# A two-layer mLSTM / Conformer step with eight experts: the three smallest experts moved into the last pass of the largest

## The chip, the cores and the metric

The kernel runs on one core of a Trainium2 chip. The metric is the device time of one execution in microseconds (us): 1841.56 is the median of three runs (1840.25 to 1843.03). Its engines are TensorE (PE; its weight loads are listed as PEld), VectorE (DVE), ScalarE (ACT), GpSimd (POOL) and SyncE (SP), which issues most transfers from device memory (DMA). Each engine runs its own instructions in order and waits on semaphores.

## What is computed

Two token groups of 128 rows (256 rows of 1024 features) pass through two layers with shared weights. Layer 0 is a bidirectional mLSTM and a dense SwiGLU; layer 1 is a convolution module and a SwiGLU with eight experts. The change concerns the experts:

```python
logits = (t @ w_router).astype(float32)              # t: tokens x 1024
top_v, top_i = lax.top_k(logits, 2)
probs = softmax(top_v)
for e in range(8):                                   # w1[e]: 1024 x 7168, w2[e]: 3584 x 1024
    u = t @ w1[e]
    out += combine[:, e:e+1] * ((silu(u[:, :3584]) * u[:, 3584:]) @ w2[e])
```

The router gives each token to two experts, 512 places in all. Only the rows that an expert was given have to be computed. All weights are float32: gate, up and down of one expert are 3 x 3584 x 1024 numbers, 44.04 MB.

## The kernel before

**Weights.** One expert's weights lie in device memory as 168 rows of 128 x 512 numbers (`EXPERT_ROWS`), in 28 stages of six rows (1536 KB). The hidden width of 3584 is cut into seven groups of 512. In order: 8 rows gate 0, 8 rows up 0, 8 gate 1, 8 up 1, 8 down 0, 8 gate 2, and so on to down 6: 21 blocks of 8 rows. SP loads the stages into `ring`, seven slots of one stage (`expert_stage`, L472).

**An ordinary pass** (`expert(i, False)`) computes one expert for up to 128 tokens. For float32 precision with fast products, each half stage (a cut of three rows) is split: ScalarE writes its rounded part to `w_hi` (L899), VectorE the rest to `w_lo` (L1349), four buffers deep, and TensorE makes three products per row, hi x hi, lo x hi and hi x lo (L1584 to L1586), of 512 columns each. A ring slot is free for the next load when its stage is split. After each group's up block come tanh on ScalarE (L942), two VectorE steps (L1455, L1456), four transposes (L1989), and the split of the hidden values (L949, L1466). The next pass's tokens are gathered by POOL from the buffer `xg` (L577) and transposed (L1910) near the end of a pass.

**Which tokens go where.** VectorE computes counts, ranks and addresses (L1382 to L1410) and the plan (L1426 to L1440). Expert 0 comes first. Of experts 1 to 7 the one with most tokens comes last and may have 192 tokens; an expert with more than its limit gets a further pass. So there are eight passes and one for each overflow.

**The last pass** (`expert(items, True)`) computes the largest expert: 128 tokens in the way above, and 64 more, the side rows, with raw float32 weights from `ring`, without a split: after each block of 8 rows `side_group` multiplies the same 8 rows (L1923), each as two products of 256 columns into the two halves of PSUM's partitions. Here a ring slot is free only when the side rows have used it (`side_rows`). The side's hidden values have their own tanh (L945), VectorE steps (L1460, L1462), two transposes (L1994) and a copy (L952). At the end the side result is copied (L1480) and stored by SP (L504); then POOL fetches each token's two results (L588), and VectorE, ScalarE and POOL combine them and do the final norm.

Of the kernel before, what the change touches and what calls it, by code (L numbers as in the profile page):

```python
# [30 lines left out]
BIG = 1e30  # L31

# [131 lines left out]
ITEMS = EXPERTS + OVER  # L164
SIDE = 64
SMALL = EXPERTS - 1
P_ITEMS, P_EXPERT, P_BIG, P_LOADS, P_ALL = 0, 1, SMALL + OVER, SMALL + OVER + 1, SMALL + OVER + 2
YG_ZERO = SMALL + 2
ZEROED = ITEMS + 1 + ITEMS + 2 - YG_ZERO


def mlstm_conformer_kernel(nc, vecs, consts, rowc, x_in, pos, w_gate, w_router, mix, ff, moe, c0, norm_out,
# [7 lines left out]
    with ctx:  # L180
# [37 lines left out]
        xg = nc.dram_tensor("xg", [(ITEMS + 1) * P, D], f32)  # L218
        yg = nc.dram_tensor("yg", [(ITEMS + 2) * P, D], f32)
# [73 lines left out]
        ranks = carve(7, EXPERTS)  # L293
        one_of = carve(4)
        side_x = carve(KD, SIDE)
        side_th, side_sg, side_tok = carve(ROW // 2), carve(ROW // 2), carve(ROW // 2)
# [11 lines left out]
        more = OVER + 1  # L308
        hit = carve(more, EXPERTS)
        hit_desc = carve(more, EXPERTS)  # L310
        has, who = carve(more), carve(more)
# [23 lines left out]

        hT_lo_end = part("hT_lo", P, KD // 2, T)
        in_hT_hi, in_hT_lo, in_w_hi = ([ring_r[:, b, MIX:STAGE].rearrange("p (k t) -> p k t", t=T) for b in blocks]
# [13 lines left out]
        BIG_UP, SIDE_UP, SIDE_Y = 1, 3, 7  # L351
# [48 lines left out]
        side_in, side_turned, side_x_ready = sem("side_in"), sem("side_turned"), sem("side_x_ready")  # L400
        side_tanh, side_chain, side_done = sem("side_tanh"), sem("side_chain"), sem("side_done")
        side_hid_turned, side_hid_ready = sem("side_hid_turned"), sem("side_hid_ready")
        side_rows = sem("side_rows")
        side_y_ready, side_y_stored = sem("side_y_ready"), sem("side_y_stored")
        xi_in, yg_stored, picked_in = sem("xi_in"), sem("yg_stored"), [sem("picked_in0"), sem("picked_in1")]
# [6 lines left out]
        def slot(n):  # L412
            return n % SLOTS
# [27 lines left out]
        def _(sp):  # L441
# [43 lines left out]
            loads = sp.value_load(plan[0:1, P_LOADS:P_LOADS + 1], min_val=SMALL - 1, max_val=SMALL - 1 + OVER)  # L485
# [7 lines left out]
            big = sp.value_load(plan[0:1, P_BIG:P_BIG + 1], min_val=1, max_val=EXPERTS - 1)  # L493
            for j in range(SLOTS):
                sp.wait_ge(split_ready, loads * CUTS + (FF_CUTS + CUTS + 2 * (j - SLOTS + 1)))
                expert_stage(None, big * FC + j, j)
            for j in range(SLOTS, FC):
                sp.wait_ge(side_rows, ((j - SLOTS) * PER + PER - 1) // KD + 1)
                expert_stage(None, big * FC + j, j)
# [1614 lines left out]
```

## Time and profile before

| | |
|---|---|
| median of three runs | 1841.56 us |
| the profiled execution | 1839.32 us, span 1837.6 us from first to last instruction |
| mean granted TensorE clock | 0.977 |
| busy: TensorE, VectorE, ScalarE | 95%, 74%, 56% of the span |
| read from device memory | 504 MB, mean 284 GB/s |
| stage loads of experts | 224 of 1536 KB |
| expert passes | from 770.46 to 1808.58 us, eight of them |

All durations below come from the one profiled execution. "Busy" for TensorE includes the modelled ends of pipelined products, so distances between starts say more than durations: an L1584 product is shown with 0.39 us, but three products follow each other in 0.68 us. A clock of 1.00 is 2.4 GHz, 0.50 would be 1.2 GHz.

### The profile page before, as it was taken

To read this page: it belongs to the slowest core of one execution; us is meant where nothing else is said; L and a number is where in the kernel's file an instruction comes from. 1 tells how busy PE (TensorE), PEld (TensorE's weight loads), DVE (VectorE), ACT (ScalarE), POOL (GpSimd) and SP (SyncE) were. 2 spreads that over 40 slices of the span, in tenths; PEclk is the share of its full clock that TensorE was granted. 3 is DMA by queue.
4 is the path that set the end of the run, shared out by engine and by line. 5 is a ranking of instruction groups with operands and counts; after the bars stand their busy time and mean duration, and the time that the engine had idled before them with its cause. 6 is when DMAs were issued, how large, how long until landed. Compare 5 with 4: busy or idle time off the path is not lost.

```text
span 1837.6 us, 25323 instructions
## 1 busy us (share of the span) xinstructions
PE 1739.5 (95%) x9456; PEld 1423.2 (77%) x9456; DVE 1362.0 (74%) x1554; ACT 1033.4 (56%) x1071; POOL 59.9 (3%) x104
## 2 busy tenths in 40 slices
PE   6999979799999999799999999999999999999993
PEld 3888858799997775588888888888888888877772
DVE  1777745556555793699999999999989999965563
ACT  2444424433342232577777777777777777754441
POOL 1011100000000000100000000000000000000001
PEclk9999999899999999899999999999999999999997
DMA  9577787245445654499999999999999999955632
GB/s 398 190 263 274 264 304 276 104 177 201 173 180 197 252 195 161 146 385 379 378 379 379 381 371 390 371 373 384 376 375 380 373 381 381 363 200 203 231 116 98
DMA packets 58930, 523.80 MB, mean 285 GB/s; under 512 B 6821, under 2 KB 7205, under 8 KB 14693
## 3 DMA queue, kind: packets, MB, share of 16 engines
q1 hardware_dynamic: 50400, 495.35, 70.2%
q0 software_dynamic: 5184, 18.62, 2.7%
q10 hardware_dynamic: 3268, 8.76, 1.2%
q8 instruction: 54, 0.88, 0.2%
q14 instruction: 24, 0.19, 0.0%
HBM read 504.08 MB, written 18.62 MB: 284 GB/s over the span
## 4 chain that ended last, share of the span: by engine, by line
PE 88%; DVE 4%; DMA 3%; ACT 2%; issue 2%; POOL 0%; DVEq 0%; SPq 0%; POOLq 0%; ACTq 0%
PE ps L1584 24%; PE ps L1586 23%; PE ps L1585 23%; PE ps L1923 4%; PE ps L1845 3%; DMA ring<-mix 2%; PE ps L1752 1%; PE ps L1835 1%; PE ps L1517 1%; PE ps L1989 1%; DVE w_lo L1349 1%; PE ps L1624 1%; DMA yg<-work 1%; ACT w_hi L899 1%; PE ps L1647 1%
## 5 line engine op out<-in xcount | busy, mean ns | idle before, releaser
L1349 DVE TENSOR_TENSOR w_lo<-ring,w_hi 128x1536 fp32r<-128x1536 f32 x448 | 778.0, 1756 | 113.9 <-ACT w_hi L899 113.4
L899 ACT ACTIVATE w_hi<-ring 128x1536 fp32r<-128x1536 f32 x448 | 668.4, 1494 | 235.9 <-PE ps L1586 227.2
L1584 PE MATMUL ps<-w_hi,hg 128*128 128x512 f32 x960 | 380.6, 396 | 11.9 <-DVE w_lo L1265 8.7
L1585 PE MATMUL ps<-w_lo,hg 128*128 128x512 f32 x960 | 376.2, 392 | 0.0
L1586 PE MATMUL ps<-w_hi,hg 128*128 128x512 f32 x896 | 350.2, 391 | 0.0
L1586 PE MATMUL ps<-w_hi,hid 128*128 128x512 f32 x624 | 244.3, 391 | 0.0
L1584 PE MATMUL ps<-w_hi,hid 128*128 128x512 f32 x560 | 220.6, 394 | 2.3 <-DVE hid L1466 2.3
L1584 PEld LDWEIGHTS ps<-w_hi,hg 128*128 128x128 f32 x960 | 181.4, 189 | 51.6 <-issue 10.6
L1585 PE MATMUL ps<-w_lo,hid 128*128 128x512 f32 x560 | 218.5, 390 | 0.0
L1585 PEld LDWEIGHTS ps<-w_lo,hg 128*128 128x128 f32 x960 | 181.4, 189 | 36.5
L1586 PEld LDWEIGHTS ps<-w_hi,hg 128*128 128x128 f32 x896 | 168.6, 188 | 35.4
L1254 DVE TENSOR_TENSOR w_lo<-ring,w_hi 128x1536 fp32r<-128x1536 f32 x56 | 96.2, 1756 | 63.1 <-ACT w_hi L829 63.1
L1586 PEld LDWEIGHTS ps<-w_hi,hid 128*128 128x128 f32 x624 | 117.9, 189 | 25.2
L1584 PE MATMUL ps<-hg,w_hi 128*128 128x256 f32 x448 | 127.4, 284 | 6.0 <-ACT gate_b L647 6.0
L1584 PEld LDWEIGHTS ps<-w_hi,hid 128*128 128x128 f32 x560 | 105.3, 188 | 28.6 <-DVE hid L1466 5.3
L1586 PE MATMUL ps<-hg,w_lo 128*128 128x256 f32 x448 | 127.3, 284 | 0.0
L1585 PEld LDWEIGHTS ps<-w_lo,hid 128*128 128x128 f32 x560 | 105.2, 188 | 20.1
L829 ACT ACTIVATE w_hi<-ring 128x1536 fp32r<-128x1536 f32 x56 | 80.6, 1484 | 65.9 <-PE ps L1586 65.9
L1584 PE MATMUL ps<-ring_r 128*128 128x256 f32 x336 | 97.1, 289 | 0.0
L1584 PEld LDWEIGHTS ps<-hg,w_hi 128*128 128x128 f32 x448 | 86.5, 193 | 7.4 <-issue 6.3
L1586 PEld LDWEIGHTS ps<-hg,w_lo 128*128 128x128 f32 x448 | 86.5, 193 | 0.0
L1317 DVE SCALAR_TENSOR_TENSOR work<-work,vec 128x256 f32<-128x256 f32 x166 | 66.4, 478 | 0.0
(292 smaller groups left out, 2140.8 us busy)
## 6 DMA issues: line engine op xcount, KB each, us to landing
ring<-moe SPq DMA_DIRECT2D x224, 1536.0 KB, 8.4
ring<-mix SPq DMA_DIRECT2D x92, 1024.0 KB, 6.7
ring<-ff SPq DMA_DIRECT2D x28, 1536.0 KB, 6.5
xg<-work POOLq DMA_DIRECT2D x12, 512.0 KB, 4.5
yg<-so ACTq DMA_DIRECT2D x9, 512.0 KB, 9.4
so<-xg POOLq DMA_DIRECT2D x7, 512.0 KB, 8.8
work<-c POOLq DMA_DIRECT2D x8, 257.0 KB, 4.6
c_out<-work ACTq DMA_DIRECT2D x8, 257.0 KB, 6.0
```

Source lines behind the costliest of these rows:

```text
L829: act.activation(w_hi[:, (2 * c + j) % W_BUFS, :], ring[:, slot(n), j * CUT * ROW:(j + 1) * CUT * ROW], ACT.Copy).then_inc(hi_ready, 1)
L899: act.activation(w_hi[:, s % W_BUFS, :], ring[:, sl, s % 2 * CUT * ROW:(s % 2 + 1) * CUT * ROW], ACT.Copy).then_inc(hi_ready, 1)
L1254: TT(w_lo[:, n % W_BUFS, :], ring[:, slot(ST_FF + c), j * CUT * ROW:(j + 1) * CUT * ROW], w_hi[:, n % W_BUFS, :].bitcast(f32), ALU.subtrac ...
L1317: ins = STT(to, src, w, to, ALU.mult, ALU.add)
L1349: TT(w_lo[:, s % W_BUFS, :], ring[:, slot(ST_MOE + s // 2), s % 2 * CUT * ROW:(s % 2 + 1) * CUT * ROW], w_hi[:, s % W_BUFS, :].bitcast(f32 ...
L1517: ins = pe.matmul(ps[32 * j:32 * j + 32, MODB, :], silu_c[:, k, :], w[:, j * ADA_COLS:(j + 1) * ADA_COLS], start=(k == 0), stop=(k == KD - 1))
L1584: pe.matmul(out, a_hi, b_hi, start=start, stop=False)
L1585: pe.matmul(out, a_hi, b_lo, start=False, stop=False)
L1586: return pe.matmul(out, a_lo, b_hi, start=False, stop=stop)
L1624: ins = pe.matmul(ps[:, MISC, j * T:(j + 1) * T], w[:, k * 256 + j * P:k * 256 + (j + 1) * P], hT[:, k, :], start=(k == 0), stop=(k == KD ...
L1845: ins = pe.matmul(ps[:, UB + s % 2, j * T:(j + 1) * T], w[:, (j * KD + k) * P:(j * KD + k + 1) * P], hT[:, k, :], start=(k == 0), stop=(k ...
L1923: ins = pe.matmul(ps[h * SIDE:(h + 1) * SIDE, bank, col * n:(col + 1) * n], tokens_64, w[:, h * n:(h + 1) * n], start=start, stop=stop)
```

## The change

Experts 1 to 7 are ranked by their counts. Rank 1 is the large expert (128 + 64 places), ranks 2 to 4 get ordinary passes (128 places), ranks 5 to 7 are small and have 64 places each. Expert 0 is first, as before. The three small experts have no pass of their own: the last pass has 21 rounds, one for each block of the large expert, and each round also has three blocks of a small one, seven rounds for one small expert. Small rows are multiplied raw, like the side rows. Two of the ring's seven slots carry the large expert's stages and five the small ones'. `STREAM` is the order in which SP loads them, `HALVES` the order in which raw blocks end, by which slots come free.

In a round m TensorE does: the split block m; the transposes of the small expert's hidden values of round m - 1; where due, those of the large expert; the side block m; three small blocks. ScalarE and VectorE have their parts in a matching order, written out by hand (`big_expert`).

```diff
-SMALL = EXPERTS - 1
+SMALLS = 3
+MIDS = EXPERTS - 2 - SMALLS
+ORDINARY = 1 + MIDS
+ITEMS = ORDINARY + OVER
+BIG_RANK, MID_RANK, SMALL_RANK = 1, 2, 2 + MIDS
+UP_BLOCK = [u // KD for u in UP_END]
+BIG_TURN = [1] + [b + 1 for b in UP_BLOCK[1:]]
+SIDE_TURN = [2] + [b + 1 for b in UP_BLOCK[1:]]
+def small_blocks(m):
+    j, q = m // GROUPS, m % GROUPS
+    if q == 0:
+        return ([(j - 1, LAST)] if j else []) + [(j, 0), (j, 1)]
+    return [(j, UP_BLOCK[q] - 1), (j, UP_BLOCK[q]), (j, UP_BLOCK[q] + 1)]
+for _m in range(BLOCKS):
+    for _w, _b in [("big", _m)] + small_blocks(_m) + ([(SMALLS - 1, LAST)] if _m == LAST else []):
+        STREAM += [(_w, st) for st in range(_b * KD // PER, (_b * KD + KD - 1) // PER + 1) if (_w, st) not in STREAM]
+BIG_SLOTS = 2
+SMALL_SLOTS = SLOTS - BIG_SLOTS
...
-            for j in range(SLOTS, FC):
-                sp.wait_ge(side_rows, ((j - SLOTS) * PER + PER - 1) // KD + 1)
-                expert_stage(None, big * FC + j, j)
+            for w, st in STREAM:
+                k, _ = place_of(w, st)
+                earlier = in_place_earlier(w, st)
+                if earlier is None:
+                    sp.wait_ge(split_ready, loads * CUTS + (FF_CUTS + CUTS + 2 * (k - SLOTS + 1)))
+                else:
+                    sp.wait_ge(halves_used, earlier)
+                expert_stage(None, experts[w] * FC + st, k)
...
-            pool.dma_start(xi[0:SIDE, :], xg[bass.ds((items + 1) * P, SIDE), :]).then_inc(side_in, 16)
+            for n in range(2):
+                if n == 0:
+                    pool.wait_ge(gathered, items + 1)
+                else:
+                    pool.wait_ge(xs_turned, 1)
+                pool.dma_start(xi, xg[bass.ds((items + (n + 1)) * P, P), :]).then_inc(xs_in, 16)
...
-            link(dve.tensor_reduce(top, key8[:, 1:EXPERTS], X, ALU.max))
-            link(TT(big, key8, top.to_broadcast([P, EXPERTS]), ALU.is_equal))
+            link(TT(above, key8.unsqueeze(1).to_broadcast([P, EXPERTS, EXPERTS]),
+                    key8.unsqueeze(2).to_broadcast([P, EXPERTS, EXPERTS]), ALU.is_gt))
+            link(dve.tensor_reduce(rank, above, X, ALU.add))
+            TS(is_big, rank, float(BIG_RANK), None, ALU.is_equal)
+            link(TS(is_small, rank, float(SMALL_RANK), None, ALU.is_ge))
...
+            def big_expert(i):          # TensorE
+                pe.wait_ge(hg_ready, i + 1)
+                for m in range(BLOCKS):
+                    for r in range(m * KD, m * KD + KD):
+                        kind, q, k, half = EXPERT_ROWS[r]
+                        if kind == "gate" and k == 0 and q >= 1:
+                            pe.wait_ge(hid_ready, i * GROUPS + q)
+                        if kind == "up" and k == 0 and q >= 1:
+                            pe.wait_ge(side_hid_ready, q)
+                        expert_row(i, r, BIG_GATE, BIG_UP)
+                        if r == CUT - 1:
+                            xs_turn(0)
+                    if m >= 1:
+                        small_turn(m - 1)
+                    if m == 1:
+                        xs_turn(1)
+                    if m in BIG_TURN[1:]:
+                        hid_turn(i, BIG_TURN.index(m), BIG_GATE)
+                    if m in SIDE_TURN:
+                        side_turn(SIDE_TURN.index(m))
+                    if m < LAST:
+                        side_block(m)
+                        if m == BIG_TURN[0]:
+                            hid_turn(i, 0, BIG_GATE)
+                        for j, b in small_blocks(m):
+                            small_block(i, j, b)
```

The first place is TensorE in the last pass. Before, in a round with a down block, the side block follows the split rows and the turns follow the side block:

```order
L1586 MATMUL ps<-w_hi,hid 128x512
L1923 MATMUL ps<-ring,xn 64x256 [waits side_hid_ready]
L1923 MATMUL ps<-ring,xn 64x256 x15
L1989 MATMUL ps<-cst,hT 128x128 [waits act_done]
L1989 MATMUL ps<-cst,hT 128x128 x3
L1994 MATMUL ps<-cst,so 128x128 [waits side_done]
L1994 MATMUL ps<-cst,so 128x128
```

Now, in such a round (L1796 is the last split product, L2197 the small expert's transposes, L2211 and L2204 the large one's, L2133 all raw products):

```order
L1796 MATMUL ps<-w_hi,hid 128x512
L2197 MATMUL ps<-cst,hT 128x128 [waits small_done]
L2197 MATMUL ps<-cst,hT 128x128
L2209 REGISTER_ALU
L2211 MATMUL ps<-cst,hT 128x128 [waits act_done]
L2211 MATMUL ps<-cst,hT 128x128 x3
L2204 MATMUL ps<-cst,so 128x128 [waits side_done]
L2204 MATMUL ps<-cst,so 128x128
L2133 MATMUL ps<-ring,xn 64x256 [waits side_hid_ready]
L2133 MATMUL ps<-ring,xn 64x256 x15
L2133 MATMUL ps<-ring,xn 64x256 [waits small_hid_ready,xs_ready,loaded6]
L2133 MATMUL ps<-ring,xn 64x256 x3
```

The turns stand ahead of the side block, two transposes are new in every round, and behind the side block come 48 more raw products, which wait themselves for their stages (`loaded6` and so on).

The second place is SP at the start of the last pass. Now the third large stage waits for a raw block and stands ahead of two small ones:

```order
L560 ISA [waits split_ready]
L560 DMA ring<-moe 128x3072
L560 ISA [waits halves_used]
L560 DMA ring<-moe 128x3072
L588 REGISTER_ALU
L560 ISA [waits split_ready]
L560 DMA ring<-moe 128x3072
```

Before, all seven first stages waited for splits only; from the eighth on each waited for `side_rows`.

The third place is ScalarE in a round with an up block. Now (L1107 is the large expert's tanh, L1071 the copy of the small one's hidden values, L1052 the splits, L1123 the side's tanh, L1066 the small one's):

```order
L1107 ACTIVATE hT<-ps 128x512 [waits u_done]
L1071 ACTIVATE so<-ps 128x256 [waits small_turned]
L1051 REGISTER_ALU
L1052 ACTIVATE w_hi<-ring 128x1536 [waits stage_used]
L1050 REGISTER_ALU
L1051 REGISTER_ALU [waits loaded1]
L1052 ACTIVATE w_hi<-ring 128x1536 [waits stage_used]
L1051 REGISTER_ALU
L1052 ACTIVATE w_hi<-ring 128x1536 [waits stage_used]
L1123 ACTIVATE so<-ps 128x256 [waits halves_used]
L1066 ACTIVATE so<-ps 128x256 [waits small_done,halves_used]
```

Before, the side's tanh stood directly behind the large one's, and the splits followed; now the splits for the next round stand ahead of both small steps.

## Rows read from the trace of the kernel before

**Rows 1.** Page, parts 1 and 2: TensorE, and the DMA in 40 slices
```profile
PE 1739.5 (95%) x9456; PEld 1423.2 (77%) x9456; DVE 1362.0 (74%) x1554; ACT 1033.4 (56%) x1071; POOL 59.9 (3%) x104
...
DMA  9577787245445654499999999999999999955632
GB/s 398 190 263 274 264 304 276 104 177 201 173 180 197 252 195 161 146 385 379 378 379 379 381 371 390 371 373 384 376 375 380 373 381 381 363 200 203 231 116 98
```

**Rows 2.** Table by stretch: busy by engine; last are clock, DMA share, GB/s
```profile
10.00:20.00 10.00, 3.13 (x15) 2.37 (x12) 3.21 (x4) 2.30 (x3) 1.75 (x6) 1.00 1.02 422
770.00:775.00 5.00, 4.54 (x13) 3.59 (x14) 4.68 (x9) 3.34 (x4) 4.19 (x3) 0.66 0.79 319
900.00:1000.00 100.00, 100.00 (x454) 82.71 (x453) 93.55 (x67) 77.66 (x61) 0.00 (x0) 1.00 0.98 377
1700.00:1750.00 50.00, 50.00 (x314) 35.84 (x315) 31.04 (x26) 24.93 (x23) 0.00 (x0) 1.00 0.59 224
1750.00:1800.00 50.00, 50.00 (x311) 35.93 (x308) 27.98 (x23) 21.24 (x20) 0.00 (x0) 1.00 0.25 95
```

**Rows 3.** Timeline (start us, us, engine, line): gathers, and the last pass's start
```profile
1480.92 0.53 POOL L577 DMA_DIRECT2D so<-xg  x1 [118.84 <-PE ps L1910]
...
1598.55 1.04 PE L1910 MATMUL ps<-cst,so 128*128 128x128 f32 x8
1600.24 0.55 POOL L580 DMA_DIRECT2D so<-xg  x1 [118.79 <-PE ps L1910]
1607.39 0.19 PEld L1584 LDWEIGHTS ps<-w_hi,hg 128*128 128x128 f32 x1
```

**Rows 4.** Timeline: the end of the last pass
```profile
1808.58 0.69 DVE L1480 COPY xn<-ps 128x512 f32<-128x512 f32 x1 [12.40 <-PE ps L1923]
```

**Rows 5.** Timeline of TensorE in the last pass; products between L1584 rows left out
```profile
1623.28 3.67 PE L1923 MATMUL ps<-ring,so 128*64 128x256 f32 x32
1626.88 0.50 PE L1584 MATMUL ps<-w_hi,hg 128*128 128x512 f32 x1
...
1632.55 3.67 PE L1923 MATMUL ps<-ring,so 128*64 128x256 f32 x32
1636.15 0.66 PE L1989 MATMUL ps<-cst,hT 128*128 128x128 f32 x4
...
1637.87 0.47 PE L1584 MATMUL ps<-w_hi,hg 128*128 128x512 f32 x1 [0.83 <-ACT xn L952]
...
1656.39 0.66 PE L1989 MATMUL ps<-cst,hT 128*128 128x128 f32 x4
...
1657.02 0.48 PE L1584 MATMUL ps<-w_hi,hg 128*128 128x512 f32 x1
```

**Rows 6.** The expert stages' tile: all loads, and their time to landing
```profile
L472 SPq DMA_DIRECT2D ring<-moe x224: 327/333/343, 675.9 to 1761.1; - x112
...
DMA to landing us min/median/max: 6.0/8.4/10.9
```

**Rows 7.** Groups of ScalarE, 1615 to 1800 us: busy us, mean ns | idle before
```profile
L899 ACT ACTIVATE w_hi<-ring 128x1536 fp32r<-128x1536 f32 x50 | 74.5, 1490 | 51.8 <-PE ps L1586 51.8
...
L945 ACT ACTIVATE so<-ps 128x256 f32<-128x256 f32 x7 | 2.7, 387 | 20.3 <-PE ps L1923 20.3
```

**Rows 8.** The same of VectorE
```profile
L1349 DVE TENSOR_TENSOR w_lo<-ring,w_hi 128x1536 fp32r<-128x1536 f32 x51 | 89.7, 1758 | 52.3 <-ACT w_hi L899 52.3
...
L1460 DVE SCALAR_TENSOR_TENSOR so<-so,ps 128x256 f32<-128x256 f32 x7 | 3.0, 422 | 4.9 <-ACT so L945 4.7
```

**Rows 9.** DMA issues from 1700 to 1790 us: count, KB each, median us to landing
```profile
ring<-moe SPq DMA_DIRECT2D x9, 1536.0 KB, 6.3
```

**Rows 10.** Timeline of VectorE: one routing step, and its first expert step
```profile
766.14 0.17 DVE L1403 TENSOR_TENSOR so<-so 128x16 f32<-128x16 f32 x1
...
769.18 1.23 DVE L1417 TENSOR_TENSOR hg<-ps,hg 128x1024 fp32r<-128x1024 f32 x1 [1.51 <-ACT hg L915]
```

**Rows 11.** Page, part 6: the ordinary token blocks' gathers
```profile
so<-xg POOLq DMA_DIRECT2D x7, 512.0 KB, 8.8
```

More of the change, by code:

```diff
@@ L31 @@
 BIG = 1e30
+BIG_KEY = 1e6
 SLOTS = 7
@@ L957, in expert, with big_high @@
                         expert_high(i, s)
-            expert(0, False, FIRST_CUTS)
+            def big_high(i, first, end):
+                for s in range(first, end):
+                    k, turn = place_of("big", s // 2)
+                    sl = slot(ST_MOE + k)
+                    if s % 2 == 0:
+                        act.wait_ge(loaded[sl], i * (16 * FC // SLOTS) + 16 * ((ST_MOE + k) // SLOTS + turn + 1))
+                    act.wait_ge(stage_used, i * CUTS + (ST_MOE + s - W_BUFS + 1))
+                    act.activation(w_hi[:, s % W_BUFS, :], ring[:, sl, s % 2 * CUT * ROW:(s % 2 + 1) * CUT * ROW],
+                                   ACT.Copy).then_inc(hi_ready, 1)
@@ L1372, in _ @@
             expert_low(0, 1)
-            count, is_over, rank, order = (over[:, n, :] for n in range(4))
-            key8, big, cap, slots, base, jump, moved = (ranks[:, n, :] for n in range(7))
-            top, big_desc, items = one_of[:, 0:1], one_of[:, 1:2], one_of[:, 2:3]
-            desc0, number = desc[:, 0, :], iota[:, 0:EXPERTS]
+            count, is_over, total, order = (over[:, n, :] for n in range(4))
+            key8, rank, is_big, is_small, cap, base, ahead, jump, shift = (ranks[:, n, :] for n in range(9))
+            extra = one_of[:, 0:1]
+            desc0 = desc[:, 0, :]
             def row_bc(a):
@@ L1444, in expert @@
+            def expert(i, begun=0):
                 for s in range(CUTS + 1):
@@ L1471, in expert, with big_low @@
                         expert_low(i, s)
-            expert(0, False, FIRST_CUTS)
+            def big_low(i, first, end):
+                for s in range(first, end):
+                    sl = slot(ST_MOE + place_of("big", s // 2)[0])
+                    dve.wait_ge(hi_ready, i * CUTS + (FF_CUTS + s + 1))
+                    TT(w_lo[:, s % W_BUFS, :], ring[:, sl, s % 2 * CUT * ROW:(s % 2 + 1) * CUT * ROW],
+                       w_hi[:, s % W_BUFS, :].bitcast(f32), ALU.subtract).then_inc(split_ready, 1)
@@ new lines, in expert_row @@
+            def expert_row(i, r, gate_bank, up_bank):
+                kind, q, k, half = EXPERT_ROWS[r]
+                s = r // CUT
+                if r % CUT == 0:
+                    pe.wait_ge(split_ready, i * CUTS + (FF_CUTS + s + 1))
+                w = (s % W_BUFS, (r % CUT) * ROW)
+                if kind == "down":
+                    if (k, half) == (0, 0):
+                        pe.wait_ge(hid_ready, i * GROUPS + (q + 1))
+                        if q == 0:
+                            pe.wait_ge(y_ready, i + 1)
+                    c = slice(k * P, (k + 1) * P)
+                    ins = product(ps[:, YB + half, :], hid_hi[:, q % 2, c], hid_lo[:, q % 2, c], w,
+                                  (q, k) == (0, 0), (q, k) == (GROUPS - 1, GC - 1))
+                else:
+                    bank = up_bank if kind == "up" else gate_bank
+                    ins = product(ps[:, bank, :], hg_hi[:, k, :], hg_lo[:, k, :], w, k == 0, k == KD - 1)
+                if r % CUT == CUT - 1:
+                    ins.then_inc(stage_used, 1)
+                if r in UP_END:
+                    ins.then_inc(u_done, 1)
```

421 lines of the change are left out of this document (274 added, 147 removed).

## The prediction

> **What bounds the kernel now.** I read the page from the top: busy shares first, then the 40 slices. TensorE is busy 95% of the span, and in the slices of the expert stage (18 to 35) the DMA engines are at 9 and 370 to 390 GB/s beside it [rows 1]. So two things stand near their limit at once, and the question is which gives way. The table by stretch splits them: in an ordinary pass (900 to 1000 us) TensorE is busy all the time with 377 GB/s beside it; in the last pass (1700 to 1750) it is busy all the time as well, but the DMA share is 0.59, and from 1750 on 0.25 [rows 2]. The last pass is therefore long because of TensorE alone, and its transfers have slack.
>
> Next the lengths. POOL issues the gather of the next token block once a pass: 1480.92 and 1600.24, so an ordinary pass takes 119.3 us [rows 3]. The last pass runs from 1607.39 to the copy of the side result at 1808.58: 201.2 us [rows 3, 4]. Its pattern is in the timeline of TensorE [rows 5]: a block of 8 rows of raw float32 products with 64 tokens takes 3.60 us (1623.28 to 1626.88), then 8 rows of split products take until 1632.55, 5.67 us with the change of kind. 21 times 9.27 is 194.7; the turns of the hidden values make up the rest. There are 28 loads for each of 8 experts (224), so no expert overflowed into a pass of its own [rows 6].
>
> **Does the change apply.** Running the reference's router on the reference's inputs gives 31, 77, 165, 54, 43, 60, 69 and 13 places for experts 0 to 7. Of 1 to 7 the largest is expert 2 (165, limit 192), the three smallest have 13, 43 and 54 (limit 64), the others 60, 69, 77 (limit 128). So there is no overflow: 8 passes become 5, four ordinary ones and the last.
>
> **Removed:** three ordinary passes, 3 x 119.3 = 358.0 us, and the old last pass, 201.2: 559.2 us in all.
>
> **Added:** a last pass of 21 rounds. A round is 8 rows of split products of the large expert, its 64 extra places on the same rows, and 24 rows for a small expert: one split block and four raw blocks.
> - Split block with the change of kind: 5.67. Four raw blocks of 3.60: 14.40 [rows 5].
> - Two transposes for the small expert's hidden values: six take 0.63 (1656.39 to 1657.02), so 0.21 [rows 5].
> - Together 20.28, times 21: 425.9.
> - The large expert's own turns, 7 times six transposes: 4.4. Two token blocks of eight transposes, 1.04 each as the ordinary gather [rows 3]: 2.1.
> That is a floor of 432.4 us. The small blocks' own product has no row before, but it is the same instruction with the same shapes as the side product. In a run of three its change of kind is paid once, which could make it 0.1 cheaper per round; waits that are met could cost as much. Exposed waits: the one of the old pass is 0.83 us (1637.87) [rows 5]. Between 0 and 0.83 a round, 0 to 17 us, I take 0.5, 10.5 in all, since most new waits have one or two blocks ahead of them but there are seven a round where there were two. The pass is 443 us.
>
> Is the chain beside it covered? After a small up block ScalarE's tanh (0.39) and two VectorE steps (0.42 each) must end before TensorE's transposes [rows 7, 8]. Behind that block stand a down block (3.6) and the next split block (5.4); where the up block is the last of a round, 5.4 remain against about 1.6. The copy back (0.39) has the side block, 3.6, as cover. ScalarE has in a round 2.7 splits of 1.49 and under 3 us else, VectorE 2.7 of 1.76 and under 4 [rows 7, 8]: neither is half full. If ScalarE waits there for a large expert's stage, the small tanh is queued behind it, but TensorE needs those same splits before it can come to the transposes, so this adds no wait of its own.
>
> **Transfers.** A stage is 1536 KB, 1.573 MB [rows 6]; a round needs 16/3 stages. The fastest stretch here, 10 to 20 us, moved 422 GB/s [rows 2]: 3.73 us a stage, 19.9 a round, below TensorE's 20.6 (432.4 / 21). The ordinary passes moved 377 at share 0.98 [rows 2]: 4.17, or 22.3 a round, above it. They were issued only as buffers came free, so 377 is a demand met, not a ceiling. I take TensorE as the bound, nearer to 422. At the start only 5 of 7 slots fill ahead, since the queue of SP stands at a wait for the first side block; the DMA engines idle for about 10.5 us (split block 5.7, the token block's turn 1.0, side block 3.6). That hides behind what was loaded ahead.
>
> What is late next is the large expert's stage. Its two slots are freed by the side block, and three small blocks (10.8 us) later TensorE wants the next rows. Landing 6.3 where transfers are sparse [rows 9] (all of them 8.4, longest 10.9) [rows 6], split 1.49 and 1.76, and my allowance of 0.5 for the issue and the handovers: ready after 10.1. A stage has six rows and a block eight, so in one round of three the new stage is wanted by the block's first row (slack 0.7), in the other two by its third or fifth, at 0.68 a row 1.4 and 2.7 us later. SP takes its loads in order, but the small stages behind are wanted by the small blocks of the next round, over 7 us later than they land.
>
> **Start and end.** The routing on VectorE gets about three instructions more of 0.17 before the addresses; it idles 1.51 before its first expert step, waiting for ScalarE [rows 10], which covers them. The plan behind it grows by three: 0 to 0.5. The token block for the last pass is 512 KB instead of 256; the ordinary one lands after 8.8 [rows 11], which from 1600.8 is about when the first three rows are done, 0 to 1. The end: 1808.58 to 1837.6 stays [rows 4]; the last small result goes out through ScalarE's queue in place of the side result, -1 to +1. I take 0 for all four.
>
> **Sum.** 559.2 - 443 = 116 us less. The profiled execution took 1839.32 (span 1837.6), so it becomes 1723; the median of the runs is 1841.56, 2.2 above, and I give 1726.
>
> **Rivals.**
> 1. *Transfers become the bound.* For: full slices now, and five passes' time for eight passes' bytes. Against: 422 GB/s at the start, and slices of 390 in the expert stage [rows 1, 2]. Of 112 stages 5 are there at the start and the last waits for a block of the last round, so 106 are in the stream. At 377 GB/s: 10.5 + 106 x 4.17 + 10 (two raw blocks and the waits behind the last landing) = 462.5: 1745. The Trainium skill (DMA: Bandwidth & Descriptors, Where 436 GB/s comes from) says that for transfers from HBM some 358 GB/s bind. The trace disagrees: 377 over a whole pass and 422 at the start are more. By the page the pass would be an estimated 486 us and the kernel 1769.
> 2. *The two slots of the large expert are too few.* With a landing of 8.4 the stage is ready at 12.2: 1.4 late in one round of three, 10 in all: 1736. With 10.9 it is ready at 14.7: 3.9, 1.2 and 2.5 late, 7.6 per three rounds, 53 in all: 1779. For: several loads are in flight when it is issued. Against: by then those of the last round have mostly landed.
> 3. *TensorE loses its clock: slower.* Where TensorE waited between short bursts for its splits (770 to 775) the granted clock was 0.66, a mix of 2.4 and 1.2 GHz [rows 2]. At 1.2 GHz the 432 us of work take twice that. Over 27% of the pass at the lower level (116 of 432) eats the gain; at 35% the kernel is at 1726 + 151 = 1877. For: more and more varied waits. Against: the old last pass has the same alternation and one wait of 0.83, and its clock is 1.00 [rows 2, 5].
> 4. *It does not do what it says:* a small expert overflows and costs a pass of 119.3: 1845. Against: 54 is ten below the limit, and no rounding moves ten tokens.
>
> **Chances.** Forecast (1716 to 1735) 0.52; transfers 0.22; slots 0.17; clock 0.05; overflow 0.01; the rest (below 1716, or mixtures) 0.03. The range 1715 to 1765 takes in the floor of 432, the transfers at 377 GB/s and the slots up to a landing of 9.8; beyond it lie the long landings and the clock. Faster by more than 0.2% (3.7 us, what a measurement here can tell) 0.94, within it 0.01, slower 0.05.
>
> **What the profile after would show.** The loads stay 224, POOL's gathers drop from 7 ordinary ones to 4 and two for the last pass. The last pass starts near 1249 and ends near 1692; rounds start 21 us apart; raw blocks take 3.60, or 10.8 for three in a run. DMA runs at 390 to 400 GB/s in it. If SP hardly waits for raw products and TensorE idles in front of small blocks, rival 1 holds. If TensorE idles in front of the split block, in one round of three most, rival 2 holds. A granted clock below 1.00 is rival 3. I am wrong if the raw block is over 3.7 us in a run of three, or if a round has over 1 us of idle time.

## The result, and the profile after

The changed kernel takes 1713.26 us (median of four runs, 1710.25 to 1715.25) against 1842.3 of the kernel before on the same chip: a ratio of 0.9295 (0.9274 to 0.9317). The forecast was 1726, with a range from 1715. The time lies 12.7 us below the forecast and 1.7 below the range.

The two profiled executions took 1839.32 (span 1837.6) and 1710.25 (span 1708.5): 129.1 us less, where the sum said 116. The page after, the answer to [rows 1]:

```profile
PE 1608.8 (94%) x9902; PEld 1282.4 (75%) x9902; DVE 1045.5 (61%) x1366; ACT 769.8 (45%) x901; POOL 57.2 (3%) x99
...
DMA  9577768445554655339999999999878999999994
GB/s 396 196 267 262 265 254 344 172 148 185 185 185 148 274 218 192 146 136 395 373 386 375 373 388 372 376 381 375 329 314 362 412 414 424 409 414 411 390 402 148
```

TensorE's share is as before (94% for 95%). The tail of half empty DMA slices is gone: seven of the last ten slices move over 400 GB/s, where those of the ordinary passes move 372 to 395. The timeline gives the stages. Columns as in [rows 3]:

```profile
760.63 0.80 PE L1794 MATMUL ps<-w_hi,hg 128*128 128x512 f32 x1 [2.37 <-DVE hg L1593]
...
1113.02 0.53 POOL L669 DMA_DIRECT2D so<-xg  x1 [118.81 <-PE ps L2120]
...
1232.33 0.53 POOL L676 DMA_DIRECT2D so<-xg  x1 [118.79 <-PE ps L2120]
...
1239.67 0.39 PE L1794 MATMUL ps<-w_hi,hg 128*128 128x512 f32 x1
...
1680.10 0.60 ACT L1079 ACTIVATE xs_a<-ps 128x512 f32<-128x512 f32 x1 [6.68 <-PE ps L2133]
```

The kernel before made its first expert product here:

```profile
770.46 0.53 PE L1584 MATMUL ps<-w_hi,hg 128*128 128x512 f32 x1 [2.37 <-DVE hg L1417]
```

| stage | before | after | difference | forecast |
|---|---|---|---|---|
| start to the first expert product | 770.46 | 760.63 | -9.8 | 0 |
| ordinary passes (7, now 4) | 836.9 | 479.0 | -357.9 | -358.0 |
| last pass, first product to the copy of the side result | 201.2 | 440.4 | +239.2 | +241.8 |
| that copy to the end of the span | 29.0 | 28.4 | -0.6 | 0 |

So the ordinary passes are as forecast: their gathers are again 119.3 apart (1113.02, 1232.33) [rows 3]. Most of the miss is in a stage to which the prediction gave nothing, and 8 us of it near 265 us, almost 500 us ahead of the first expert.

**The start.** The kernel before, ScalarE and POOL at the end of the mLSTM:

```profile
262.83 0.63 POOL L555 DMA_DIRECT2D yg<-work  x1
...
265.03 1.07 PE L1517 MATMUL ps<-ring,silu_c 128*32 128x512 f32 x8 [1.29 <-DMA ring<-mix]
...
273.65 0.63 ACT L807 ACTIVATE hg<-so 128x512 fp32r<-128x512 f32 x1 [6.83 <-DMA yg<-work]
```

The same places after:

```profile
227.02 0.62 POOL L647 DMA_DIRECT2D yg<-work  x1
...
265.75 0.63 ACT L904 ACTIVATE hg<-so 128x512 fp32r<-128x512 f32 x1 [0.42 <-DVE so L1302]
```

POOL fills the token buffers `xg` and `yg` with zeros, one block of 512 KB in each turn of the mLSTM, and ScalarE waits for all of them (`act.wait_ge(xg_zeroed, 16 * ZEROED)`, L799 before, L896 after) ahead of its first copy into `hg`. With fewer expert passes the buffers are smaller: 13 blocks in place of 16. The last fill went out at 262.83 and ScalarE's copy starts 10.8 us later; now it goes out at 227.02, and ScalarE waits only 0.42, for VectorE. The copy is 7.9 us earlier. A wait of TensorE for weights (1.29) is gone as well in this profile; it is 0.43 in another of the same kernel (number 5), and that the fill slowed that load is not shown. Of the 9.8, 1.7 more are the router's products, before and after:

```profile
749.61 5.30 PE L1866 MATMUL ps<-hT,wr 128*8 128x256 f32 x16 [2.25 <-ACT hT L639]
```

```profile
741.78 3.61 PE L2076 MATMUL ps<-hT,wr 128*8 128x256 f32 x16 [1.91 <-ACT hT L736]
```

The granted clock was 0.66 there before (750 to 755 us) and 0.99 after (740 to 745). This is not the change's doing: the changed kernel profiled again (number 5) has 5.30, and the kernel before with its fills moved (number 1) has 3.61.

**The last pass.** Table by stretch, the changed kernel, columns as in [rows 2]:

```profile
1260.00:1300.00 40.00, 35.50 (x270) 24.79 (x270) 8.82 (x12) 6.44 (x10) 0.00 (x0) 0.96 0.84 346
1300.00:1400.00 100.00, 99.52 (x770) 69.07 (x768) 33.58 (x34) 26.55 (x32) 0.00 (x0) 1.00 1.00 418
1400.00:1500.00 100.00, 99.21 (x766) 68.50 (x764) 32.23 (x31) 26.01 (x30) 0.00 (x0) 1.00 1.00 415
1500.00:1600.00 100.00, 97.01 (x743) 66.85 (x740) 28.78 (x30) 23.81 (x30) 0.00 (x0) 1.00 0.98 407
```

TensorE is busy 99% of 200 us while the DMA engines are at a share of 1.00. From 1300 to 1500 us neither has room left. A round, in TensorE's timeline (products between rows left out; the answer to [rows 5]):

```profile
1426.61 0.50 PE L1794 MATMUL ps<-w_hi,hg 128*128 128x512 f32 x1 [0.46 <-DVE w_lo L1656]
...
1432.23 0.38 PE L2197 MATMUL ps<-cst,hT 128*128 128x128 f32 x2
1432.54 3.67 PE L2133 MATMUL ps<-ring,xs_a 128*64 128x256 f32 x32
1436.05 7.08 PE L2133 MATMUL ps<-ring,xn 128*64 128x256 f32 x64
1442.95 3.62 PE L2133 MATMUL ps<-ring,so 128*64 128x256 f32 x32
1446.51 0.50 PE L1794 MATMUL ps<-w_hi,hid 128*128 128x512 f32 x1
```

The round takes 19.90 us (1426.61 to 1446.51). Its four raw blocks take 13.97 together, 3.49 each, not the 3.60 of [rows 5]: behind another raw block there is no change of kind. The waits of TensorE for VectorE in the pass (engine, line, waited for: us in total, times, longest):

```profile
PE ps L1794 <- DVE w_lo L1656: 5.8, 7, 2.2
...
PE ps L1794 <- DVE hid L1631: 4.5, 1, 4.5
```

The one wait of 4.50 is at 1282.88, in the round of the first hidden values:

```profile
1267.21 0.66 PE L2211 MATMUL ps<-cst,hT 128*128 128x128 f32 x4
...
1276.49 2.86 ACT L1052 ACTIVATE w_hi<-ring 128x1536 fp32r<-128x1536 f32 x2 [11.76 <-DMA ring<-moe]
...
1279.52 0.59 ACT L1090 ACTIVATE hid<-ps 128x512 fp32r<-128x512 f32 x1
...
1282.14 0.69 DVE L1631 TENSOR_TENSOR hid<-ps,hid 128x512 fp32r<-128x512 f32 x1
...
1282.88 0.79 PE L1794 MATMUL ps<-w_hi,hg 128*128 128x512 f32 x1 [4.50 <-DVE hid L1631]
```

The transposes are issued at 1267.21, but ScalarE copies their result at 1279.52: in its program two splits stand ahead of the copy, and they wait 11.76 for a load. Right behind the wait, from 1282.88 to 1290.04, the granted clock is 0.76; over the stretch of 40 us it is 0.96.

### The profile page after: what moved, and what is told of

Same layout as the page of the kernel before. It is cut to its first block, busy times and chain, and to the rows that moved or that the text cites. A ratio compares the mean times of both kernels' runs of the same rounds, so it can differ in the third digit from the quotient of the medians.

```text
span 1708.5 us, 25100 instructions
## 1 busy us (share of the span) xinstructions
PE 1608.8 (94%) x9902; PEld 1282.4 (75%) x9902; DVE 1045.5 (61%) x1366; ACT 769.8 (45%) x901; POOL 57.2 (3%) x99
## 4 chain that ended last, share of the span: by engine, by line
PE 79%; DMA 9%; DVE 6%; ACT 4%; issue 2%; POOL 1%; DVEq 0%; SPq 0%; ACTq 0%; POOLq 0%
PE ps L1794 18%; PE ps L1796 18%; PE ps L1795 18%; PE ps L2133 9%; DMA ring<-moe 7%; PE ps L2055 3%; PE ps L1962 2%; PE ps L1727 2%; DMA ring<-mix 2%; PE ps L2045 1%; DVE w_lo L1656 1%; ACT w_hi L1052 1%; PE ps L1834 1%; DVE w_lo L1521 1%; PE ps L2211 1%
## 5 line engine op out<-in xcount | busy, mean ns | idle before, releaser
L1521 DVE TENSOR_TENSOR w_lo<-ring,w_hi 128x1536 fp32r<-128x1536 f32 x224 | 388.4, 1756 | 32.7 <-ACT w_hi L996 32.3
L996 ACT ACTIVATE w_hi<-ring 128x1536 fp32r<-128x1536 f32 x224 | 334.3, 1495 | 102.9 <-PE ps L1796 98.5
L1794 PE MATMUL ps<-w_hi,hg 128*128 128x512 f32 x624 | 249.6, 400 | 14.9 <-DVE w_lo L1656 5.7
L1656 DVE TENSOR_TENSOR w_lo<-ring,w_hi 128x1536 fp32r<-128x1536 f32 x56 | 96.7, 1756 | 267.6 <-ACT w_hi L1052 267.6
L1795 PE MATMUL ps<-w_lo,hg 128*128 128x512 f32 x624 | 245.4, 393 | 0.0
L1796 PE MATMUL ps<-w_hi,hg 128*128 128x512 f32 x560 | 219.8, 392 | 0.0
L1052 ACT ACTIVATE w_hi<-ring 128x1536 fp32r<-128x1536 f32 x56 | 81.1, 1482 | 229.3 <-DMA ring<-moe 226.6
L1796 PE MATMUL ps<-w_hi,hid 128*128 128x512 f32 x456 | 178.6, 392 | 0.0
L1794 PE MATMUL ps<-w_hi,hid 128*128 128x512 f32 x392 | 154.9, 395 | 1.4 <-DVE hid L1631 1.3
L1794 PEld LDWEIGHTS ps<-w_hi,hg 128*128 128x128 f32 x624 | 118.4, 190 | 46.0 <-DVE w_lo L1656 9.8
L1426 DVE TENSOR_TENSOR w_lo<-ring,w_hi 128x1536 fp32r<-128x1536 f32 x56 | 96.2, 1757 | 63.0 <-ACT w_hi L926 63.0
L1796 PE MATMUL ps<-hg,w_lo 128*128 128x256 f32 x448 | 127.9, 286 | 0.0
L2133 PE MATMUL ps<-ring,xn 128*64 128x256 f32 x1120 | 124.2, 380 | 0.6 <-ACT so L1071 0.6
L1796 PEld LDWEIGHTS ps<-w_hi,hg 128*128 128x128 f32 x560 | 105.9, 189 | 22.5
L2133 PEld LDWEIGHTS ps<-ring,xn 128*64 128x64 f32 x1120 | 80.6, 137 | 40.4 <-issue 1.9
L926 ACT ACTIVATE w_hi<-ring 128x1536 fp32r<-128x1536 f32 x56 | 80.6, 1484 | 65.9 <-PE ps L1796 65.9
L2133 PE MATMUL ps<-ring,xs_a 128*64 128x256 f32 x896 | 100.2, 381 | 0.0
L1796 PEld LDWEIGHTS ps<-w_hi,hid 128*128 128x128 f32 x456 | 86.1, 189 | 18.5
```

Of the source, the lines that this page charges most:

```text
L926: act.activation(w_hi[:, (2 * c + j) % W_BUFS, :], ring[:, slot(n), j * CUT * ROW:(j + 1) * CUT * ROW], ACT.Copy).then_inc(hi_ready, 1)
L996: act.activation(w_hi[:, s % W_BUFS, :], ring[:, sl, s % 2 * CUT * ROW:(s % 2 + 1) * CUT * ROW], ACT.Copy).then_inc(hi_ready, 1)
L1052: act.activation(w_hi[:, s % W_BUFS, :], ring[:, sl, s % 2 * CUT * ROW:(s % 2 + 1) * CUT * ROW], ACT.Copy).then_inc(hi_ready, 1)
L1426: TT(w_lo[:, n % W_BUFS, :], ring[:, slot(ST_FF + c), j * CUT * ROW:(j + 1) * CUT * ROW], w_hi[:, n % W_BUFS, :].bitcast(f32), ALU.subtrac ...
L1521: TT(w_lo[:, s % W_BUFS, :], ring[:, slot(ST_MOE + s // 2), s % 2 * CUT * ROW:(s % 2 + 1) * CUT * ROW], w_hi[:, s % W_BUFS, :].bitcast(f32 ...
L1656: TT(w_lo[:, s % W_BUFS, :], ring[:, sl, s % 2 * CUT * ROW:(s % 2 + 1) * CUT * ROW], w_hi[:, s % W_BUFS, :].bitcast(f32), ALU.subtract).th ...
```

## The experiments

Each was compared with the kernel before on the chip that it ran on. Where a stage is read from a profile, the start has to be set apart: the last mLSTM state is stored at 250.44 and 250.45 us in the two kernels' profiles, but at 252.1 to 256.7 in those of all twelve experiments, whatever their code (256.16 in number 5, which is the changed kernel itself). Why is open. The length of the last pass is therefore given below from POOL's gather ahead of it to the copy of the side result; it is 447.8 us in the profile above, and 449.5 (number 5) and 445.1 (number 2) in two others with the same code there.

### 1 and 2: the zero fills

The kernel before, with three fills issued ahead of the loop:

```diff
+            for n in range(3):
+                pool.dma_start(xg[n * P:(n + 1) * P, :], zeros).then_inc(xg_zeroed, 16)
             for it in range(ITS):
...
-                if it < ITEMS + 1:
+                f = it + 3
+                if f < ITEMS + 1:
```

> The kernel before with the same 16 zero fills of 512 KB, but three of them issued ahead of the mLSTM loop, so that the last one goes out three turns earlier (near 227 us instead of 263). Theory A (the 10 us that the change gained ahead of the experts come from ScalarE's wait for the last zero fill, which the change takes away because it needs 13 fills and not 16): 8 to 10 us faster than before, ratio 0.995, and ScalarE's 6.8 us wait for DMA yg<-work at its hg copy is gone. Rival B (they come from the smaller number of bytes, or from somewhere else in the changed program): no change, ratio 1.000.

Measured: 1835.84 against 1843.72, ratio 0.9959 (0.9944 to 0.9973), 7.9 us less with an interval of 5.0 to 10.3. ScalarE's wait is gone:

```profile
272.59 0.63 ACT L810 ACTIVATE hg<-so 128x512 fp32r<-128x512 f32 x1 [0.42 <-DVE so L1133]
```

The changed kernel, with sixteen fills again:

```diff
-XG_BLOCKS, YG_BLOCKS = ITEMS + 3, ITEMS + 4
+XG_BLOCKS, YG_BLOCKS = ITEMS + 3, ITEMS + 7
```

> The changed kernel with 16 zero fills instead of 13, the last three going to rows of the result buffer that nothing reads, at the same turns as before the change. Theory A: the wait is back, 8 to 10 us slower than the changed kernel (about 1722, ratio 0.935), and the first expert's first product stands near 770 instead of 760.6. Rival B, if the bytes matter little and the gain lies elsewhere: 1713, ratio 0.930.

Measured: 1725.76 (1721.49 to 1733.06), ratio 0.9379 (0.9358 to 0.94). The wait is back:

```profile
267.41 0.63 POOL L647 DMA_DIRECT2D yg<-work  x1
...
278.83 0.63 ACT L904 ACTIVATE hg<-so 128x512 fp32r<-128x512 f32 x1 [7.66 <-DMA yg<-work]
```

This cost 12.5 us by the medians (9.1 against the changed kernel measured again, number 5), at the upper end of what was expected or above it; of the 11.2 us between the profiles 4.6 lie ahead of the last state's store and are there already at the fourth fill (116.47 for 111.95), before the fills differ. From that store to the copy it takes 23.2 and 23.8 us in the two kernels with late fills, and 15.3 to 16.2 in all others. So the late fills are shown in both directions: 7 to 8.5 us by the copy's place, 7.9 by the first experiment's times, 9 to 12 by the second's. Number 1 has all sixteen fills, so it is their place in time that counts and not their bytes (rival B). It is the part of the gain that the prediction did not have: with sixteen fills the kernel takes 118.0 us less than the one before on the same chip, where 116 were forecast. That the medians fall on the forecast as well (1725.76 and 1726) is partly luck, since terms of the last pass cancel (below).

### 3: the copy of the hidden values ahead of the splits

```diff
+                        big_hid_copy(i, 0)
                     if m in BIG_TURN[1:]:
...
-                    if m == BIG_TURN[0]:
-                        big_hid_copy(i, 0)
```

(and the same for VectorE's step).

> The changed kernel with one thing moved in round 1 of the last pass: ScalarE's copy and VectorE's subtraction of the first hidden values (L1090, L1631) stand ahead of the splits of the next block's rows, not behind them. Theory C (the longest wait of the last pass, 4.5 us at 1282.88, arises because that copy is queued behind two splits that wait 11.8 us for a load of the large expert): the wait falls to under 1.5 us, the slow clock behind it goes too, 4 to 6 us faster than the changed kernel, about 1708. Rival D (the split rows themselves come too late there, so TensorE would wait for them anyway): under 1.5 us gained.

Measured: 1711.43 (1710.87 to 1713.81), ratio 0.9288 (0.9274 to 0.9302). ScalarE now copies right behind the transposes:

```profile
1272.74 0.60 ACT L1090 ACTIVATE hid<-ps 128x512 fp32r<-128x512 f32 x1 [3.16 <-PE ps L2208]
```

but TensorE's waits for the splits grew from 5.8 to 8.0:

```profile
PE ps L1791 <- DVE w_lo L1655: 8.0, 8, 2.2
```

The pass takes 444.4 us, 0.7 to 5.1 less than in the three profiles of the unchanged pass. The wait of 4.5 is gone, as Theory C said, and part of it comes back at the loads; what is gained is less than expected and not to be told from none by the times (1713.26 and 1716.69 for the kernel unchanged).

### 4: three slots for the large expert

```diff
-BIG_SLOTS = 2
+BIG_SLOTS = 3
```

> The changed kernel with three ring slots for the large expert and four for the small ones instead of two and five. Rival 2 of the prediction (two slots are too few: the waits of 2.2 and 2.1 us in front of split blocks at 1550.95 and 1614.59, with ScalarE waiting 12.4 us for a load there): these waits go, 4 to 7 us faster. Theory E (the transfers run at their limit, 415 GB/s at a share of 1.00, and a slot given to the one is taken from the other): the waits move to the small blocks, no change or up to 6 us slower.

Measured: 1846.27 (twelve runs, 1837.83 to 1851.64), ratio 1.0012 (0.9999 to 1.0026): 133 us more than with two. Neither theory had a number near this. Waits of TensorE, and one stretch:

```profile
PE ps L1794 <- DVE w_lo L1656: 59.8, 17, 5.1
...
PE ps L2133 <- DMA ring<-moe: 37.4, 20, 3.2
```

```profile
1400.00:1500.00 100.00, 78.91 (x544) 53.97 (x542) 28.03 (x27) 22.48 (x26) 0.00 (x0) 0.91 0.78 322
```

TensorE waits for both kinds of load while the DMA engines idle for a fifth of the time. So it is not the rate: the loads are issued too late. By the code a round needs four small stages, and with four slots for them the last must wait for the first small block of its own round; SP issues in order, and the large expert's next load stands behind it. Number 10 tests this.

### 5: the changed kernel again

> The changed kernel as it is, as the partner on the same chip for the next three. Ratio 0.930 to the kernel before, as in the first measurement.

Measured: 1716.69 (1714.67 to 1719.5), ratio 0.9319 (0.9303 to 0.9335), with a last pass of 449.5 us. So the same kernel comes out 3.4 us apart on two occasions, and a difference of that size between versions says nothing.

### 6 and 7: all seven slots filled at the start

```diff
+EARLY = [("big", 0), ("big", 1)] + [(0, _n) for _n in range(SMALL_SLOTS)]
+STREAM = EARLY + [_x for _x in STREAM if _x not in EARLY]
```

> The changed kernel with the fourth and fifth small stage loaded ahead of the third large one at the start of the last pass, so that all seven ring slots are full when TensorE starts it. Theory F (after the start the transfers are the bound: share 1.00 and 415 GB/s from 1300 to 1500 us, so two stages loaded while the DMA engines would idle come off the stream): the waits in front of split blocks in the middle (2.2 and 2.1 us) go, 3 to 7 us faster than the changed kernel. Rival G (TensorE is the bound, the waits come from the order of steps and not from bandwidth): under 1.5 us.

Measured: 1716.22 (1708.23 to 1717.46), ratio 0.9302 (0.9281 to 0.9324), pass 447.4. With the edit of number 3 beside it:

> The same together with the moved hidden copy of round 1. The last pass loses both kinds of wait, 12 us in all with the slow clock behind the first: 8 to 11 us faster than the changed kernel, near 1703. If theory F is wrong, only the 2 to 3.5 us of the hidden copy.

Measured: 1713.35 (1710.68 to 1716.67), ratio 0.9306 (0.9288 to 0.9323), pass 444.3. The early fill is worth 0 to 2 us: that the missing two loads at the start cost the pass 3 us or more (Theory F) is refuted. The prediction had said that they hide, and they do.

### 8 and 9: which of the two bounds holds the last pass

Half of each small stage's load taken away, all products kept (on old numbers):

```diff
+                    n = STAGE // 2
+                    sp.dma_start(ring[:, slot(ST_MOE + k), 0:n],
```

> The changed kernel, each small expert's stage loaded only to its first half (768 KB instead of 1536; the other half of the slot keeps old numbers, and the small experts' products run on them). TensorE's work is unchanged. If TensorE is the bound of the last pass and transfers only add waits (my forecast), it gains what TensorE idles, 7 to 12 us, most of it 1.8 us per late stage. If the transfers are the bound (rival 1) it gains 20 us or more.

Measured: 1702.93 (1699.91 to 1705.25), ratio 0.9239 (0.922 to 0.9258). One stretch:

```profile
1300.00:1400.00 100.00, 100.00 (x780) 69.84 (x778) 33.57 (x34) 26.54 (x32) 0.00 (x0) 1.00 0.69 266
```

With half of the small stages' bytes gone TensorE has no idle time in this stretch (4.1 us in the whole pass), and the pass takes 436.4, 9 to 13 less. Most of its rounds take 19.90 us, or 20.52 with the large expert's turns. That is close to TensorE's own length; what the transfers add is 9 to 13 us. The expectation's 7 to 12 for a pass bound by TensorE is met, the 20 or more for one bound by transfers is not.

The other way round, every second row of a small expert left out of the products, all loads kept:

```diff
+                    if k % 2:
+                        continue
```

> The changed kernel with only every second row of the small experts multiplied (the odd k are left out), all loads as before. TensorE has some 110 us less to do in the last pass. What is left is the floor of the transfers. By the rate seen in the middle of the pass, 415 GB/s or 3.79 us a stage: 10.5 + 106 x 3.79 + some 8 = 420 us against 441, so 18 to 24 us faster than the changed kernel, near 1692. If the transfers could really run much faster than TensorE takes them, it gains 50 us or more.

Measured: 1722.31 (1719.17 to 1727.54), ratio 0.9351 (0.9334 to 0.9368): by the ratios 6 to 10 us slower than the changed kernel (from its second and its first measurement; the interval of the second just touches this one's), with some 110 us less for TensorE to do (63 blocks of 3.49, halved). All theories had this faster. Waits of TensorE, one stretch, and one of the waits:

```profile
PE ps L1794 <- DVE w_lo L1656: 76.3, 19, 6.1
```

```profile
1400.00:1500.00 100.00, 79.61 (x511) 55.02 (x512) 25.84 (x26) 22.65 (x27) 0.00 (x0) 0.85 0.94 387
```

```profile
1420.72 3.67 PE L2133 MATMUL ps<-ring,xs_a 128*64 128x256 f32 x32
...
1431.24 2.86 ACT L1052 ACTIVATE w_hi<-ring 128x1536 fp32r<-128x1536 f32 x2 [10.03 <-DMA ring<-moe]
...
1434.56 0.79 PE L1794 MATMUL ps<-w_hi,hg 128*128 128x512 f32 x1 [4.99 <-DVE w_lo L1656]
```

The pass takes 453.6 us. What TensorE saved it now waits for the large expert's stage (76.3 us; for small stages 2.5), and its granted clock over the stretch is 0.85 instead of 1.00.

This is not the floor of the transfers that the experiment was made for: 420 us was the estimate from their rate, and the DMA engines are not at their limit here (387 GB/s at a share of 0.94). The rows show a closed loop instead. The side block (1420.72 to 1424.22) frees a slot; the next large stage is there for ScalarE's split at 1431.24, 7.0 us later, near the 6.3 of [rows 9]; 3.3 later, at 1434.56, TensorE starts the split block; that takes 7.9 at the slow clock and the next side block ends at 1446.32. Together that is 22.1 us, and 453.6 over 21 rounds is 21.6. With two slots for the large expert the loop has no slack, so work taken from the small blocks turns into waiting. How much of it is the slots and how much the clock was not separated.

### 10 to 12: the large expert's loads issued by POOL

Three slots as in number 4, but from the fourth stage on issued by POOL, so that they do not stand behind SP's:

```diff
-BIG_SLOTS = 2
+BIG_SLOTS = 3
...
+            for st in range(BIG_SLOTS, FC):
+                k, _ = place_of("big", st)
+                pool.wait_ge(halves_used, in_place_earlier("big", st))
+                pool.dma_start(ring[:, slot(ST_MOE + k), :],
```

> Three large and four small slots as in the experiment that lost 133 us, but the large expert's loads from the fourth on are issued by GpSimd and not by SP. Theory H (the 133 us come from SP's one queue: the last small stage of a round waits for a block of the same round, and the next large stage is stuck behind it): most of it comes back, under 1760. Theory I (four small slots are too few by themselves, since a stage is loaded only 2 blocks before it is wanted): still over 1800, TensorE waits in front of small blocks.

Measured: 1807.24 (1804.96 to 1812.39), ratio 0.9812 (0.9797 to 0.9827). Only the small loads are waited for now:

```profile
PE ps L2145 <- DMA ring<-moe: 77.8, 20, 7.6
```

So of the 133 us of number 4 about 40 come back, and the waits for the large expert's stages are gone: that part is the queue's order. Theory I has its signs, over 1800 us and TensorE waiting in front of small blocks; Theory H's 1760 is missed. But loads from POOL cost 25 to 29 us by themselves (number 11), so the order may be worth more than 40, and what four small slots cost is not separated from it. The same with two and five slots:

> Two large and five small slots as in the changed kernel, the large expert's loads issued by GpSimd. If the order in SP's queue costs the late large stages, 2 to 6 us faster; if bandwidth does, within 2 us of the changed kernel; the descriptors that GpSimd writes itself could also make the landings longer and cost up to 10.

Measured: 1744.09 (1739.96 to 1748.58), ratio 0.9453 (0.9439 to 0.9467), by the ratios 25 to 29 us slower than the changed kernel, where at most 10 was expected:

```profile
PE ps L1806 <- DVE w_lo L1668: 29.4, 14, 4.5
```

```profile
1500.00:1600.00 100.00, 88.43 (x636) 60.00 (x634) 28.04 (x27) 22.49 (x26) 2.64 (x5) 0.91 0.86 355
```

With number 3's edit as well:

> The same with the hidden copy of round 1 moved ahead. As e11, and 2 to 3.5 us faster than it.

Measured: 1741.84 (1734.01 to 1746.89), ratio 0.9457 (0.9444 to 0.947). By the times this is no different from number 11; the 2 to 3.5 us are not seen.

A queue of its own does not make the large expert's stages arrive in time. One by one they land fast, after a median of 6.8 us from POOL's issue. But one round in three needs two of them, and POOL issues them together:

```profile
1432.67 1.13 POOL L684 DMA_DIRECT2D ring<-moe  x2 [19.34 <-PE ps L2145]
```

The split of the first starts at 1440.54, that of the second at 1447.91, 15.2 us after the issue and 7.4 after the first; in the changed kernel the second split of such a pair starts 3.7 after the first (1423.28 and 1426.94). In number 11 these rounds take 24.5 to 26.8 us, all others but two 19.9 to 21.2. The rate fell from 407 GB/s to 355 in the stretch above. Whether the second stage is late through POOL's way of issuing, or because two queues share the DMA engines, was not separated.

No version that computes the same result beats the changed kernel by more than its own scatter (0.9295 and 0.9319): the nearest are number 3 (0.9288), number 6 (0.9302) and number 7 (0.9306).

## Why the prediction was wrong

**The step that failed** is "Start and end": "I take 0 for all four". It looked at the routing, the plan, the token block and the last result, and these are near 0 (the routing a few tenths, the end -0.6). The fifth item is not in it: the constants `ITEMS` and `ZEROED`, which count the zero fills that ScalarE waits for in the mLSTM. The row that gives it away was in the trace before, ScalarE idle for 6.83 on `DMA yg<-work`. Numbers 1 and 2 show it in both directions. With it the sum would have had 7 to 8 us more gain, the forecast would have been near 1718 and the range would have begun near 1707, with the 1713.26 inside. The range had nothing below 1715 because all its uncertainty was put into the last pass. The rest of the 13 us between the profiles is smaller: 1.7 is the clock at the router's products, which comes and goes between executions, 2.6 the last pass and 0.6 the end.

**Removed, ordinary passes:** right, 119.3 us each.

**The last pass:** 443 forecast, 440.4 measured. The parts were near, and two of them erred against each other. The raw blocks are 3.49 instead of 3.60 (four a round: -0.43, -9 over 21 rounds); the sentence on the change of kind had this at 0.1 a round, on three blocks, and did not take it into the sum. A round of 19.90 less 13.97 leaves 5.93 for split block and transposes (5.88 forecast). 21 rounds of 19.90, with the 4.4 for the large expert's turns and 2.1 for two token blocks, make 424. Of the 16 above that, 11.3 are recorded waits (10.3 in front of split blocks, 1.0 for the small expert's steps; 10.5 were allowed), some 1.6 the slower clock behind the largest (the split block that starts at 1282.88 takes 7.2, the one at 1426.61 takes 5.6), and about 3 are not assigned. So the raw blocks gave back 9 us that waits beyond the allowance, the clock and the unassigned rest mostly took: that the pass came out 2.6 from the forecast is partly luck. The allowance was nearly right as a sum and wrong in kind: not a half microsecond a round, but one of 4.5 and seven of up to 2.2.

**Is the chain beside it covered:** for the small experts yes, TensorE's waits for their steps are 1.0 us in all. Not for the large expert's first hidden values (1282.88): the prediction weighed ScalarE's waits for a load only against the small tanh, not against a copy that TensorE wants before the splits behind it.

**Transfers (rival 1, 0.22):** not the bound, but as near as TensorE. "377 is a demand met, not a ceiling" was right: 415 to 418 GB/s for 200 us. But the DMA share is 1.00 there. At that rate a round's 16/3 stages take 20.1 to 20.2 us, and TensorE's rounds take 19.90, or 20.52 with the large expert's turns (number 8), 20.1 in the mean. The two bounds coincide; the prediction's 19.9 against 20.6 us a round was the right picture with the two still apart. Number 8 puts what the transfers add at 9 to 13 us. Number 9 does not measure them. The Trainium skill (DMA: Bandwidth & Descriptors, Where 436 GB/s comes from) has some 358 GB/s binding for transfers from device memory, which it works out as half of the 716 of two cores, and 435 as the ceiling of the transfer fabric. For one core with no other running the trace disagrees with the first, with 418 GB/s over 100 us; no slice of the page is above the second.

**Two slots too few (rival 2, 0.17):** its sign is there, at less than its price. The waits stand where it said, most of them in one round of three (1365, 1427, 1492, 1551 and 1615 us), but come to 5.8 us where its first sum had 10. All loads issued from 1260 to 1660 us land after a median of 12.2 us, longer than the 10.9 with which it came to 53 us:

```profile
ring<-moe SPq DMA_DIRECT2D x101, 1536.0 KB, 12.2
```

That median is not the large stages': SP issues those right behind the side block, and ScalarE can split them 6.6 to 9.9 us after that block's end in the rounds from 1290 on (side block over at 1436.05, split at 1445.39), near the 8.4 of its first sum. The 12.2 are mostly of small stages, which stand behind each other and are wanted later. In number 9, where TensorE came earlier, TensorE waits for the large stage 19 times (76.3), so this loop is what holds the pass next. A third slot taken from the small ones is no cure (number 4).

**Clock (rival 3):** it fell only behind the longest wait (0.76 over the 7 us that follow it) and was 1.00 in the stretches of 100 us; in numbers 4, 9 and 10, with long waits in each round, it is 0.85 to 0.93 in the stretches of 100 us. The mechanism is there, its condition was not met by the changed kernel. **No overflow (rival 4):** right, five passes.

**What it had named as tests:** the pass starts at 1239.67 for 1249 and ends at 1680.10 for 1692 (both shifted by the start); rounds are 21.0 apart in the mean (440.4 / 21); DMA is at 407 to 418 for 390 to 400. Of the two signs of being wrong it named, the raw block over 3.7 us is absent (3.49), but idle time over 1 us in a round is there in three of 21 rounds (4.5, 2.2 and 2.1), though 0.5 in the mean.

## What to carry to other kernels

A change to the number of passes or items changes everything that is counted by that number: list all constants derived from it, find each wait on them, and look for its row in the trace of before, far from the code that the change is about. Where two resources are both near full, take half of the work away from one and see what the other gives: half of the small loads gone gave 9 to 13 us. It only measures the other resource if nothing else closes a loop; half of the small products gone gave no gain at all, because the loop through the large expert's two slots then took 21.6 us a round. In a ring shared by two streams and filled by one in-order queue, count the slots for one round of each stream before moving one over: one slot moved cost 133 us.

## What the runs showed of the hardware

- One core held 415 to 418 GB/s over 200 us beside a TensorE busy 99%, with landings of 12.2 us (median, 1536 KB, 1260 to 1660 us) against 6.3 where transfers are sparse [rows 9].
- Taking 110 us of work from TensorE made the kernel no faster, by the ratios 6 to 10 us slower (number 9), with a granted clock of 0.85 to 0.91 in the last pass's stretches in place of 1.00.
- The same large loads issued by POOL while SP issued the small ones: 25 to 29 us slower, 355 GB/s in place of 407 from 1500 to 1600 us (number 11), with the second of two stages issued together split 7.4 us after the first in place of 3.7.
- A 64-column raw block of 32 products takes 3.49 us in a run of such blocks and 3.60 between split ones.
- The point at which the last mLSTM state is stored moves by 5.7 us between two profiles of the same kernel (250.45, and 256.16 in number 5), and sixteen products of the router take 3.61 us in one and 5.30 in the other.
